# First projections from an unnormalised stream behind three norms, and another order of the start, in a two-layer hybrid transformer kernel

## What is computed

```python
h  = layer_norm(x) * (1 + mod[1]) + mod[0]          # modulations differ for latent and context tokens
y  = token_mixer(h @ w_in[l]) @ w_out[l]            # neighbourhood attention (A), GQA (B), HGRN2 (C)
x  = layer_norm(ALPHA * x + mod[2] * y, ln1_g[l], ln1_b[l])
f  = conv_ffn(layer_norm(x) * (1 + mod[4]) + mod[3], w_up[l], ...)   # width-3 convolution, silu gate
x  = layer_norm(ALPHA * x + mod[5] * f, ln2_g[l], ln2_b[l])
```

## Time and profile before

| what | us |
|---|---|
| median of 3 runs (lowest, highest) | 3637.96 (3637.43, 3638.48) |
| the profiled execution | 3641.97 |
| its span, first to last instruction | 3639.8 |
| TensorE busy in it | 3432.4 |
| mean granted TensorE clock | 0.979 |

### The profile page before, as it was taken

How to read it: one execution, slowest core, us unless ns; L and a number is a source line. 1 busy time by engine, 2 the same in 40 slices (tenths; PEclk the granted TensorE clock), 3 DMA queues, 4 the chain that set the end, 5 groups by cost and what they waited for, 6 DMA issues and landing times.

```text
span 3639.8 us, 57152 instructions
## 1 busy us (share of the span) xinstructions
PE 3432.4 (94%) x24613; PEld 2827.6 (78%) x24613; DVE 1618.0 (44%) x2601; ACT 1004.5 (28%) x1438; POOL 1076.3 (30%) x412
## 2 busy tenths in 40 slices
PE   6999999979989999999999899999979899999998
PEld 5777778867768888888886677788867678888887
DVE  4333563056166334334334533463086564434436
ACT  4334564124132111111112333464133221111111
POOL 1212101302333333333333212201312444444443
PEclk9999999999999999999999999999989999999999
DMA  5111001352201111111112111000162111111111
GB/s 182 37 27 30 1 2 50 97 187 58 66 24 35 39 37 35 37 39 36 41 35 76 23 24 27 24 2 24 35 193 76 52 41 52 46 47 47 52 47 64
DMA packets 269678, 186.41 MB, mean 51 GB/s; under 512 B 45405, under 2 KB 249077, under 8 KB 269429
## 3 DMA queue, kind: packets, MB, share of 16 engines
q1 hardware_dynamic: 268272, 182.28, 16.7%
q10 hardware_dynamic: 1156, 0.48, 0.1%
HBM read 174.33 MB, written 8.39 MB: 50 GB/s over the span
## 4 chain that ended last, share of the span: by engine, by line
PE 83%; DVE 9%; issue 3%; ACT 2%; POOL 1%; DMA 1%; ACTq 0%; POOLq 0%; DVEq 0%; PEldq 0%
PE psum L1032 60%; PE psum L891 6%; PE psum L1132 5%; PE psum L1282 3%; PE psum L900 2%; PE psum L1210 2%; DVE f_t L2281 1%; PE psum L1058 1%; DVE y_chan L2172 1%; DVE c_x L2136 1%; PE psum L960 1%; PE psum L1241 1%; DVE h_lo L1931 1%; ACT f_t L2816 1%; PE psum L1366 1%
## 5 line engine op out<-in xcount | busy, mean ns | idle before, releaser
L1032 PE MATMUL psum<-h_hi,w_split 128*128 128x512 f32 (+1 forms) x5952 | 1437.7, 370 | 18.3 <-POOL w_split L846 8.1
L844 POOL TENSOR_SCALAR w_split<-w_raw 128x1024 fp32r<-128x1024 f32 x196 | 552.0, 2816 | 2390.4 <-PE psum L1032 1653.1
L1032 PEld LDWEIGHTS psum<-h_hi,w_split 128*128 128x128 f32 x5952 | 1030.3, 188 | 223.7 <-issue 12.0
L1032 PE MATMUL psum<-h_lo,w_split 128*128 128x512 f32 (+1 forms) x2976 | 799.9, 368 | 0.0
L1032 PEld LDWEIGHTS psum<-h_lo,w_split 128*128 128x128 f32 x2976 | 516.0, 188 | 97.6
L2281 DVE SCALAR_TENSOR_TENSOR f_t<-psum,vec,f_t 128x1023 f32<-128x1023 f32 (+1 forms) x264 | 260.2, 1013 | 705.4 <-ACT f_t L2816 702.3
L846 POOL TENSOR_TENSOR w_split<-w_raw,w_split 128x1024 fp32r<-128x1024 f32 x196 | 477.0, 2434 | 16.4
L1032 PE MATMUL psum<-f_hi,w_split 128*128 128x512 f32 (+1 forms) x1696 | 416.9, 371 | 15.7 <-DVE y_chan L2172 10.7
L2816 ACT ACTIVATE f_t<-psum,vec 128x1280 f32<-128x1280 f32 (+1 forms) x88 | 115.4, 1311 | 910.2 <-PE psum L1032 886.7
L1032 PEld LDWEIGHTS psum<-f_hi,w_split 128*128 128x128 f32 x1696 | 295.9, 188 | 80.3 <-issue 25.0
L2172 DVE SCALAR_TENSOR_TENSOR y_chan<-psum,mods,y_chan 128x1024 f32<-128x1024 f32 (+1 forms) x256 | 247.2, 1003 | 172.2 <-PE psum L1032 171.8
(11 more groups left out here) (275 smaller groups left out, 3471.6 us busy)
## 6 DMA issues: line engine op xcount, KB each, us to landing
w_raw<-in_w_up_dram SPq DMA_DIRECT2D x88, 512.0 KB, 3.8
ada_late<-in_w_ada_dram SPq DMA_DIRECT2D x32, 1024.0 KB, 7.3
w_raw<-in_w_down_dram SPq DMA_DIRECT2D x44, 512.0 KB, 3.8
w_raw<-in_w_in_dram SPq DMA_DIRECT2D x42, 512.0 KB, 3.9
ada<-in_w_ada_dram SPq DMA_DIRECT2D x4, 2048.0 KB, 17.9
ada_early<-in_w_ada_dram SPq DMA_DIRECT2D x8, 1024.0 KB, 5.3
x_first<-in_x_dram SPq DMA_DIRECT2D x8, 512.0 KB, 12.6
o_x<-in_x_dram SPq DMA_DIRECT2D x8, 512.0 KB, 3.9
```

Source lines behind the costliest of these rows:

```text
L844: pool.tensor_scalar(w_hi[:, n % 2], w_raw[:, n % 2], 1.0, None, ALU.mult).then_inc(s["w_hi_done"], 1)
L1032: last = pe.matmul(columns(key, t0, t0 + tn), weight, a[:, k, t0:t0 + tn], start=(k == order[0] and j == 0), stop=(k == order[-1] and j == 2))
```

## The change

**Behind each norm.** Layer norm is linear in the stream apart from factors per token. So the first two weight tiles of a stage are now multiplied with the raw stream, scaled only per channel (ln_a): ScalarE writes the high half (`raw_high`), VectorE the low half (`raw_low`, signals z_ready), while the last output tile or the last down products still run. `raw_gemms` takes the place of PE's `norm_tail` and of the first interleaved pair. Between its k steps it makes the last statistics, the turned sums, 16 products of the shift rows with the unsplit weights (`shift_products`), the broadcasts (`spread_two`, now in pieces of 512 or 256 tokens with semaphores of their own) and the first corrections; `close` adds a rank-24 product of shift rows and token rows. The missing factor per token is applied to the result: in F by VectorE in PSUM (`scaled`), in A by VectorE as it copies a_k and a_v out (`raw_part`, ScalarE's work before). The tiles that are multiplied from the normed stream are now the second FFN pair (the second of them two k steps behind, lag 2), or a_q alone. Convolution, silu and gate of the first pair stand inside VectorE's and ScalarE's loops over the channel tiles. The `end_phase` barriers at the ends of O and F of layer 0, and of O of layer 1, become `leave`. The moments' broadcasts for the residual go between the k steps of the fifth FFN tile. VectorE works out three more per-token values with reciprocals and widens the shift rows (`widen_setup`).

**The start.** SyncE loads all ten token tiles, then ada 0, a_k and a_v, ada 2, the masks, ada 1 and 3. VectorE normalises the tokens first and takes the parameter rows behind them; ScalarE makes the conditioning vector between two tokens. The modulations are folded in two halves: channels 0 to 511 before the first channel tile, the rest between the products of the second. The engines leave the first phase ahead of k = 3.

The diff, cut to its core:

```diff
-            for n, tokens in enumerate((range(0, 3), range(3, 6), range(6, NT), ())):
-                load_ada(n)
-                for i in tokens:
-                    load_first(i)
-                if n == 1:
-                    sp.dma_start(masks_in[:], level_masks).then_inc(s["masks_landed"], 16)
...
+                    for st, raw in enumerate(RAW_TILES):
+                        if plan.tiles[n - 2] in raw:
+                            sp.wait_ge(s["raw_shift"], st + 1)
...
+            for i in range(NT):
+                load_first(i)
+            load_ada(0)
             weights_up_to("in", 0, COL["a_v"])
+            load_ada(2)
+            sp.dma_start(masks_in[:], level_masks).then_inc(s["masks_landed"], 16)
+            for n in (1, 3):
+                load_ada(n)
...
-                pool.wait_ge(*freed("bc", st, 0))
-                for k in range(1, KT, 2):
+                done, many = spreads(st)
+                pool.wait_ge(s["bc_taken"], done + many)
+                for n, k in enumerate(range(1, KT, 2)):
                     if k >= 3:
                         pool.wait_ge(s["hk_ready"], KT * st + k - 1)
-                    pool.tensor_tensor(kt_[:, 1, 0:w], y_chan[:, k, 0:w], r_b[:, 0:w], ALU.mult).then_inc(s["kt_ready"], 1)
+                    pool.tensor_tensor(kt_[:, 1, 0:w], y_chan[:, k, 0:w], r_of(st)[:, 0:w], ALU.mult).then_inc(s["kt_ready"], 1)
+                    if n < len(tiles):
+                        split_up_to(*tiles[n])
...
+            def normed_gemms(st, tiles, keys, parts, lag):
+                many = len(pieces(q_tiles(STAGES[st][0])))
+                for k in range(KT + lag * (len(tiles) - 1)):
                     if k < KT - 2:
                         for n in range(2):
                             correct(st, k + 2, n)
-                    if k >= 0:
+                    if k < KT:
                         wait((s["hk_ready"], KT * st + k + 1))
                     for at_, (tile, key) in enumerate(zip(tiles, keys)):
-                        if at_ == 1 and many == 3 and k < KT - 2:
+                        n, own_k = plan.tile[tile], k - lag * at_
+                        if 0 <= own_k < KT:
+                            if own_k == 0:
+                                wait((s["w_ready"], n + 1))
+                                wait(before(*key))
+                            last = gemm_step(n, slot(*key), own_k, parts)
+                            if own_k == KT - 1:
+                                fill(last, *key)
+                        if at_ == 0 and many == 3 and k < KT - 2:
...
+            def raw_gemms(st, left):
+                l, which = STAGES[st]
+                done, many = spreads(st)
+                tiles, keys = raw_tiles(st), raw_keys(st)
+                parts = GROUPS[:many]
+                def last_sums():
+                    left()
+                    statistics(st, KT - 1)
+                def shift_products():
+                    wait((s["set_widened"], st + 1))
+                    wait((s["set_taken"], 2 * st + 2))
+                    wait((s["var_ready"], 2 * st + 1))
+                    if st == 0:
+                        wait((s["xt_taken"], 3 * KT))
+                    for t, tile in enumerate(tiles):
                         n = plan.tile[tile]
+                        wait((s[f"w_landed{n % 2}"], w_counts[n]))
+                        weight = w_raw[:, n % 2].rearrange("p (k n) -> p k n", k=KT)
+                        for k in range(KT):
+                            last = pe.matmul(psum[64 * t:64 * t + 56, 6, 3 * P:4 * P], set_wide[:, k, :], weight[:, k],
+                                             start=(k == 0), stop=(k == KT - 1))
+                    last.then_inc(s["raw_shift"], 1)
+                def spread_two(first):
+                    def run():
+                        for n in (first, first + 1):
+                            kind, (t0, tn, _), bank = spread_piece(st, n)
+                            if n >= 2:
+                                wait((s["bc_taken"], done + n - 1))
+                            wait((s["cols_ready"], st + 1) if kind else (s["gain_col"], st + 1))
+                            if n == 1:
+                                wait((s["raw_shift_taken"], st + 1))
+                            for i in range(t0 // P, (t0 + tn) // P):
+                                c_ = stat_place(q_tiles(l), i)
+                                src = colmat[:, c_] if kind else al[:, 15, c_:c_ + 1].broadcast_to([P, P])
+                                last = turn(psum[:, bank, P * i - t0:P * i - t0 + P], src)
+                            last.then_inc(s["bc_full"], 1)
+                    return run
+                def close(t):
+                    wait((s["raw_shift_taken"], st + 1))
+                    wait((s["bc_taken"], done + 2 * many))
+                    for t0, tn, who in pieces(q_tiles(l)):
+                        rows_ = slice(64 * t + 32 * who, 64 * t + 32 * who + 24)
+                        last = pe.matmul(slot(*keys[t])[:, t0:t0 + tn], raw_vec[rows_, :], ranks_of(st)[rows_, t0:t0 + tn],
+                                         start=False, stop=True)
+                    fill(last, *keys[t])
+                def corrections(k, of):
+                    def run():
                         if k == 0:
-                            wait((s["w_ready"], n + 1))
-                            wait(before(*key))
-                        last = gemm_step(n, slot(*key), k, parts)
-                        if k == KT - 1:
-                            fill(last, *key)
+                            wait((s["bc_taken"], done + 2 * many))
+                        for n in of:
+                            if n < many:
+                                correct(st, k, n)
+                    return run
+                def close_first():
+                    close(0)
+                    corrections(0, (2,))()
+                gemm(tiles[0], keys[0], parts, ready=lambda k: (s["z_ready"], KT * st + k + 1),
+                     between={2: last_sums, 4: lambda: sum_columns(st), 6: shift_products}, fills=False, closes=False)
+                between = {n: spread_two(2 * n) for n in range(many)}
+                between.update({3: corrections(0, (0, 1)), 4: close_first, 5: corrections(1, (0, 1)), 6: corrections(1, (2,))})
+                gemm(tiles[1], keys[1], parts, between=between, used=s["z_used"], fills=False, closes=False)
+                close(1)
...
+            for i in range(NT):
+                if i == 4:
+                    turn_rows()
+                turn_normed(("h", 0, i))
+            wait((s["cond_ready"], 1))
+            for n in (0, 2):
                 first_modulations(n)
-                for i in tokens:
-                    turn_normed(("h", 0, i))
-            fold_modulations(1, 1)
-            end_phase(pe, (s["mods_full"], 1), "h0")
+            fold_modulations(1, 0)
...
+                    wait((s["mods_ready"], 1))
+                    first_modulations(1)
                     for k in range(KT):
+                        if k == 1:
+                            first_modulations(3)
+                        if k == 3:
+                            leave(pe, (s["mods_full"], 2), "h0")
                         wait((s["first_ready"], k + 1))
                         for name in "kv":
+                            if (k, name) == (1, "v"):
+                                fold_modulations(2, 1)
...
-                    norm_tail(2 * l - 1)
-                    normed_gemms(2 * l - 1, [("in", l, COL["a_" + name]) for name in "kv"], [("A", l, r, name) for name in "kv"])
-                    first = 2
+                    raw_gemms(2 * l - 1, lambda: leave(pe, full("Y", l - 1, NPAIR - 1, KT - 1), "F", l - 1))
+                    normed_gemms(2 * l - 1, [("in", l, COL["a_q"])], [("A", l, r, "q")], groups(l), 0)
+                    first = 3
...
-                norm_tail(2 * l)
-                normed_gemms(2 * l, [("up", l, 0, half) for half in range(2)], [("F", l, 0, half) for half in range(2)])
-                spread_moments(l)
+                raw_gemms(2 * l, lambda: leave(pe, full("W", l, KT - 1), "O", l))
+                normed_gemms(2 * l, [("up", l, 1, half) for half in range(2)], [("F", l, 1, half) for half in range(2)],
+                             groups(l), 2)
+                moments_at = {2 * n + 1: spread_moments(l, 2 * n) for n in range(len(pieces(q_tiles(l))))}
                 if l == DEPTH - 1:
-                    spread_gates(l)
+                    moments_at[7] = partial(spread_gates, l)
...
+                    if k == 3:
+                        first_modulations(1)
+                        leave(dve, (s["mods_ready"], 2), "h0")
...
+            def raw_low(st, k):
+                dve.wait_ge(s["z_hi"], KT * st + k + 1)
+                for a, b, who in [(0, LAT, 0)] + [(LAT, T, 1)] * (q_tiles(STAGES[st][0]) == NT):
```

(46 more changed lines are left out.)

434 lines of the change are left out of this document (264 added, 170 removed).

## The result

The changed kernel takes 3648.42 us (median of 7 runs, 3646.78 to 3651.47) against 3637.96 us for the one before (median of 7 too, 3634.08 to 3643.53); the ratio is **1.0026**, 95% interval [1.0016, 1.0036]. It is slower by 0.26%, some 9.5 us by the ratio (10.5 between the medians), where 9 us were forecast the other way; 3648.4 also lies outside the range of 3616 to 3643. The profiled execution has a span of 3645.4 us, 5.6 more than before.

The account below looks back on a forecast made before the run. TensorE is busy for 94% of the span, so only its standstills and lower-clock stretches can give time. +0.8 - 8.5 + 1.6 - 3 = -9.1 us gives 3632.9 profiled, 3629 as median; range 3616 to 3643.

Parts of the forecast that it names:

- Start (+0.8): Start of layer 0: first product 9.5 us earlier, but the later bias table makes the first scores 0.8 us later.
- Norm 0 (-8.5): Norm between output projection and FFN of layer 0: 8.5 us gained, bounds 20 and 2 gained.
- End: E + 83.7: Norm of layer 0 ahead of the FFN: loop's end at E + 82.0, plus 1.2 for a collision and 0.5 for the clock.
- E: TensorE's end of the last product ahead of a norm: 998.80 before layer 0's FFN, 1986.40 between the layers.
- the prediction's own pair: VectorE's low half at 1085.33, taking 2.88 us in place of 1.49 beside GpSimd's subtraction of 1084.46, in the kernel before.
- Norm 1 (+1.6): Norm between the layers: bias table ready at 2069.95 against first scores at 2068.32, 1.6 us lost; bounds -3 and +6.
- hk_ready 8 by the ladder at E + 66.0: Norm between the layers: last channel tile normed at 2052.4 by VectorE's order of instructions, today 2043.64.
- Norm 2 (-3): Norm of layer 1 with 8 token tiles: 71.1 us against 74.0, 3 us gained; bounds 13 and -2.
- (a): Rival, start and norm between the layers: neither bias table binds, transfers are issued faster or earlier; 29.5 us gained, 3608; 7%.
- (b): Rival, loops of both norms ahead of the FFNs: they keep up with TensorE, scalings and convolutions hidden; 3607; 9%.
- (c): Rival, norm loops: VectorE's collisions with GpSimd cost 1.0 us at each of 24 channel tiles, 24 us lost; 3653; 11%.
- the signs named ahead: First product near 47, SyncE's mask issue near 60, TensorE waiting for h_lo or kt, 12 us idle ahead of layer 1's scores.

Follow-up runs that it names:

- Experiment 3: Changed kernel with the bias over the first-half modulation weights only, SyncE waiting for these instead of the first phase's end: 1.0009 to the kernel before.
- norms_only: Changed kernel with the start of the kernel before, so that only the norms are changed: 1.0025 to the kernel before.
- after: The changed kernel itself, with the whole change against the kernel before: 3648.42 us, ratio 1.0026; its profiled execution spans 3645.4 us.
- Experiments 10 and 11: Mean-term subtraction left out of the FFN's residual (8 instructions a layer), in the changed kernel and in the kernel before: stretch from down pair 0 to 2 170.0 us in both.
- no_sub: Changed kernel without the subtraction of the mean term in the FFN's residual; executed once, no ratio: modulations of layer 0 to its last FFN pair 1058.5 us.
- experiments 3 and 4: Experiment 3, and the changed kernel with SyncE in layer 1 waiting for the fourth normed channel tile instead of the eighth: 1.0009 and 1.0004 to the kernel before.

## Why the prediction was wrong

**Start (+0.8): right, with its mechanism.** The first product came at 48.49 (46.9 said), SyncE's issues at 58.01 (60.3), the table at 107.1 (109.4), and the scores around 121 us 0.9 later than before. Experiment 3 shows the table as the cause. The first-pass reading, which engine waits for nobody today and will bind tomorrow, was worth the effort here.

**Norm 0 (-8.5): wrong, measured +3.6 (norms_only) to +5.7 (after), by b and c together.** Neither bound, 2 and 20 us gained, held it. Two steps failed.
The first is the loop, "End: E + 83.7". With E at 996.16, TensorE was through the raw part at E + 41 (38.4 said), began the two new tiles at E + 42.1 (39.8) and was ready for the next at 1086.98, E + 90.8: of the 7.1 us too many, 2.3 came ahead of the loop and 4.8 in it. With the 3.0 that the forecast has for the moments' turns still to come, 1.6 us of the gain of 8.5 were left at this point. The account took 0.5 us for the clock behind a wait of 5. In fact, behind the wait of 3.03 us at 1043.22, the granted clock was 0.51 from 1043 to 1060, the groups took 1.27 us instead of 0.74, and the wait of 1.61 fell into this stretch. Late products are then late corrections: VectorE, which I had as the engine that sets the pace, waits 3.80 us at 1060.67 for a correction behind those products. Collisions were small: the low half of 2.48 us at 1049.54 beside GpSimd's subtraction of 1048.32 is the only instruction of VectorE in the loop that one lengthened. It fits the rule of the Trainium skill (SBUF — State Buffer, Who interferes with whom) that such a pair excludes each other: 1.14 us were left of GpSimd's, 0.99 were lost. (In the prediction's own pair 1.53 us were left and 1.39 lost; it gave the 1.39 as what was left.)
The second is the end of the account. The forecast compared times at the end of the fourth tile and took what was won there for the kernel's. VectorE's work isn't done there: four residuals stood in a row, 14.8 us from 1098.90 to the low half at 1113.67, one operation of them at 3.69, and the next convolution behind them. VectorE has 14 us more to do by the second half of the first down pair than before (123.94 against 109.95: scalings, low halves and shifts of the raw part, longer collisions), and TensorE paid for it with waits of 2.71 and 2.06 us and with 1.3 more in the third. Experiments 10 and 11 show this for stretch c, where it costs 5.2 us; for the 2.71 in stretch b the wait is gone in no_sub too.

**Norm 1 (+1.6): right in kind, wrong in size, +5.2 to +9.0.** The bias table did bind, TensorE stood for 12.93 us where some 13 were to be expected (2057 to 2070). What was off is "hk_ready 8 by the ladder at E + 66.0": it came 70.5 behind the start of the raw products (1991.6), and that start itself came 2.1 late, by the set-up rows that VectorE widens ahead of the last pair; this work was not in the account. The loop's step was argued as VectorE's alone. Measured, a pair takes 9.3 us by the chain of VectorE and GpSimd and 11.0 where TensorE's clock is down, about the 10.9 that it took before with twice the products at full clock (2024.10 to 2035.01 in the trace of before). So most of the step is VectorE's and GpSimd's after all; the lower clock, at which the third piece comes late, adds up to 1.7 us a pair. And the price depends on luck on the other side: the old norm took 155.0 or 158.8 us as its clock came back sooner or later.

**Norm 2 (-3): nothing** (f: 894.2 against 894.3). The term that was mis-sized is again the loop. With E at 2855.1, where norm 2 starts in after, TensorE began the next weight tile at 2927.27, E + 72.2, where 67.8 had been forecast; 1.52 us of that were a wait for GpSimd's split of its weights, which the account doesn't have. With the 3.3 of turns to come that is 75.5, against 74.0 before. How the rest of the stretch made up for it I didn't measure.

**The rivals.** (a) was half the truth in another order: with neither table binding the change would by estimate be some 5 us faster than before (9.5 less 6.2 and 8, from experiments 3 and 4; no run has these two edits alone), not 30, because the norms' gains were not there. (b) is refuted. (c) comes nearest in time (3653) but hasn't the mechanism: collisions of 1.0 per tile are not in the rows. The side that I gave 11% was reached by VectorE's arrears and TensorE's clock, for which I had no rival at all. Of the signs named ahead, the first product, SyncE's first issue, TensorE's waits for kt and h_lo (3.03 and 1.61) and its idle time ahead of the scores came about as said; low halves over 2 us, the sign of (c), came once in the loop of norm 0.

What stays open: what decides when the clock comes back in the old norms, which leaves norm 1's price between 5.2 and 9.0; and how much of norm 0's loop would come back at full clock.
